# Attention of an encoder layer: probabilities divided by their sum before they are turned, values stationary in two column halves, no turning of the attention output

## What is computed

```python
qb = q.reshape(b, nb, ATTN_BLOCK, g, r, ATTN_HEAD_DIM)
scores = jnp.einsum('bnqgrd,bnkgd->bgrnqk', qb, kb) * (1.0 / math.sqrt(ATTN_HEAD_DIM))
scores = jnp.where(valid, scores - slopes * dist, -jnp.inf)
m = jnp.maximum(jnp.max(scores, axis=-1, keepdims=True), sink_l)
e = jnp.exp(scores - m)
p = e / (jnp.sum(e, axis=-1, keepdims=True) + jnp.exp(sink_l - m))
out = jnp.einsum('bgrnqk,bnkgd->bnqgrd', p, vb)
...
return jnp.concatenate([attn.astype(h.dtype), rec], axis=-1) @ w_out
```

## Time and profile before

| | us |
|---|---|
| median of 3 runs | 1134.76 |
| lowest, highest | 1132.54, 1134.95 |
| the profiled execution | 1135.22 |
| its span in the profile | 1133.4 |
| TensorE busy | 1052.5 (93%) |
| VectorE, ScalarE busy | 306.3 (27%), 174.4 (15%) |
| moved by DMA | 427.89 MB, mean 378 GB/s |

### The profile page before, as it was taken

One profiled execution on the slowest core, in us unless ns is written; L12 is line 12 of the kernel. 1 busy time (PEld: TensorE's weight loads), 2 busy tenths in 40 slices (PEclk: granted clock), 3 DMA queues, 4 the chain that ended last, 5 costly groups with the idle time before them and its releaser, 6 DMA issues.

```text
span 1133.4 us, 14445 instructions
## 1 busy us (share of the span) xinstructions
PE 1052.5 (93%) x5143; PEld 444.2 (39%) x5143; DVE 306.3 (27%) x775; ACT 174.4 (15%) x353; POOL 23.9 (2%) x31
## 2 busy tenths in 40 slices
PE   7999999999999999999999999999999999999996
PEld 6888756333333333333333333333333333332333
DVE  5266344222222222221222222222222222211114
ACT  2263211111111111111111111111111111111101
POOL 2500000000000000000000000000000000000000
PEclk8999999999999999999999999999999999999999
DMA  9722696998999999999999999999999999999992
GB/s 318 207 94 81 270 383 256 389 421 335 422 422 422 422 422 421 421 422 422 422 422 422 422 421 422 422 422 422 422 422 422 422 422 422 421 422 422 422 421 115
DMA packets 73539, 427.89 MB, mean 378 GB/s; under 512 B 8048, under 2 KB 21392, under 8 KB 24272
## 3 DMA queue, kind: packets, MB, share of 16 engines
q1 hardware_dynamic: 71984, 427.19, 92.3%
q10 hardware_dynamic: 1536, 0.43, 0.2%
HBM read 426.02 MB, written 1.05 MB: 377 GB/s over the span
## 4 chain that ended last, share of the span: by engine, by line
PE 56%; DMA 27%; SPq 9%; DVE 6%; issue 2%; ACT 0%; DVEq 0%; ACTq 0%
DMA ring<-in_w_up_dram 26%; PE bank L1308 21%; PE bank L1364 13%; SPq L302 8%; PE bank L1066 8%; PE bank L1273 3%; PE bank L1094 2%; DVE wbuf L991 2%; PE bank L1349 1%; DVE wbuf L986 1%; PE bank L1281 1%; DVE wbuf L995 1%; PE bank L1318 1%; DVE wbuf L985 1%; PE bank L1213 1%
## 5 line engine op out<-in xcount | busy, mean ns | idle before, releaser
L1308 PE MATMUL bank<-ring,wbuf 128*64 128x512 f32 x2032 | 460.6, 595 | 28.8 <-DMA ring<-in_w_up_dram 28.7
L1308 PEld LDWEIGHTS bank<-ring,wbuf 128*64 128x64 f32 x2032 | 140.2, 137 | 324.0 <-issue 224.8
L1364 PE MATMUL bank<-ring,wbuf 128*64 128x512 f32 x960 | 217.5, 595 | 0.0
L985 DVE TENSOR_SCALAR wbuf<-bank 128x256 f32<-128x256 f32 x64 | 26.9, 420 | 361.4 <-PE bank L1308 361.4
L1364 PEld LDWEIGHTS bank<-ring,wbuf 128*64 128x64 f32 x960 | 66.7, 137 | 124.5 <-issue 124.4
L976 DVE TENSOR_SCALAR hT<-iota_s,hT 128x64 f32<-128x64 f32 x62 | 12.9, 251 | 342.1 <-PE bank L1308 342.1
L602 ACT ACTIVATE wbuf<-wbuf 128x256 f32<-128x256 f32 x64 | 26.7, 416 | 506.8 <-DVE wbuf L985 506.8
L963 DVE TENSOR_TENSOR wbuf<-wbuf,bank 128x512 f32<-128x512 f32 x124 | 76.7, 680 | 0.0
L1288 PE MATMUL bank<-wbuf,putT 64*128 64x512 f32 x264 | 65.6, 615 | 0.7 <-ACT wbuf L612 0.7
L1066 PE MATMUL bank<-hT,wbuf 128*128 128x256 f32 x272 | 62.4, 391 | 2.4 <-ACT hT L473 2.4
L1273 PE MATMUL bank<-X,hT 128*64 128x512 f32 x256 | 62.0, 605 | 0.1
(11 more groups left out here) (235 smaller groups left out, 557.2 us busy)
## 6 DMA issues: line engine op xcount, KB each, us to landing
ring<-in_w_up_dram SPq DMA_DIRECT2D x254, 1024.0 KB, 25.2
ring<-in_w_down_dram SPq DMA_DIRECT2D x120, 1024.0 KB, 23.2
wbuf<-in_w_in_dram SPq DMA_DIRECT2D x13, 1024.0 KB, 10.5
wbuf<-in_w_out_dram SPq DMA_DIRECT2D x2, 2048.0 KB, 8.7
wbuf<-in_w_down_dram SPq DMA_DIRECT2D x4, 1024.0 KB, 5.8
mixa<-in_w_up_dram SPq DMA_DIRECT2D x2, 1024.0 KB, 14.5
mixa<-in_w_down_dram SPq DMA_DIRECT2D x2, 1024.0 KB, 9.0
cat<-in_w_down_dram SPq DMA_DIRECT2D x2, 1024.0 KB, 10.5
```

Source lines behind the costliest of these rows:

```text
L985: v.tensor_scalar(glu[:, w], pair[:, :, 0], LIMIT, None, ALU.min).then_inc(s["glu_ready"], 1)
L1308: ins = mm(bank[n][c * SLOTS:(c + 1) * SLOTS, :], xT[:, k, :], wk[:, c * FF + n * 512:c * FF + (n + 1) * 512], start=(k == 0), stop=(k == ...
L1364: ins = mm(bank[2][c * SLOTS:(c + 1) * SLOTS, :], actT[:, at:at + SLOTS], wk[:, a * D + c * 512:a * D + (c + 1) * 512], start=(i == 0 and ...
```

## The change

Each batch's exponentials are multiplied by the reciprocal of their sum on VectorE (`shared`, a 128x1024 product in place in `score`) and only then turned: `pT` waits for the new semaphore `prob_shared` and no longer for `prob_ready`. `shared(b)` stands in VectorE's order where `mixed(b)` stood for b = 0; `shared(1)` comes ahead of `q_in`, `shared(2)` ahead of `scaled(1)`, `shared(3)` ahead of `masked`. `pv` becomes two jobs, one for each token tile: `va` (64 columns of a group) is stationary, `probT` of four heads moves (512 columns), group 0 writes partitions 0 to 63 of the bank, group 1 partitions 64 to 127. The result has the heads' columns on the partitions, so the jobs `catT` 0 and 1 go; ScalarE copies the bank to `attT` (`attended`), and `w_out`'s first half is loaded with its rows in the matching order, in two DMAs of 64 partitions.

```diff
-        STEPS += [("proj", "qh", 0), ("pv", 0, 0), ("proj", "qh", 1)] + two("pT", 1) + two("score", 3)
-        STEPS += [("proj", "ih", 0), ("pv", 1, 0), ("proj", "ih", 1)] + two("pT", 2) + two("kpT", 0)
-        STEPS += [("proj", "zg", 0), ("pv", 2, 0)] + two("kpT", 1) + two("aT", 0) + two("aT", 1) + two("pT", 3)
-        STEPS += [("proj", "zg", 1), ("pv", 3, 0), ("kv", 0, 0), ("kv", 1, 0), ("catT", 0, 0), ("catT", 1, 0)]
+        STEPS += two_of("qh") + two("pT", 1) + two("score", 3)
+        STEPS += [("proj", "ih", 0), ("pv", 0, 0), ("proj", "ih", 1)] + two("pT", 2) + two("kpT", 0)
+        STEPS += [("proj", "zg", 0)] + two("kpT", 1) + two("aT", 0) + two("aT", 1) + two("pT", 3)
+        STEPS += [("proj", "zg", 1), ("pv", 1, 0), ("kv", 0, 0), ("kv", 1, 0)]
...
-            for i in range(2):
-                sp.wait_ge(s["proj_done"], len(UNITS) - 3 + 2 * i)
-                sp.dma_start(wbuf[:, 1 + i, :].rearrange("p (k n) -> p k n", k=4),
-                             w_out_v[:, 4 * i:4 * i + 4, :]).then_inc(s["wout_in"], 16)
-            sp.wait_ge(s["attn_cat"], len(BATCH))
+            sp.wait_ge(s["proj_done"], len(UNITS) - 3)
+            for g in range(NG):
+                sp.dma_start(wbuf[g * DH:(g + 1) * DH, 1, :].rearrange("p (k n) -> p k n", k=QPG),
+                             w_out[0][g * QPG * DH:(g + 1) * QPG * DH, :].rearrange("(k p) n -> p k n", p=DH)).then_inc(s["wout_in"], 16)
+            sp.wait_ge(s["proj_done"], len(UNITS) - 1)
+            sp.dma_start(wbuf[:, 2, :].rearrange("p (k n) -> p k n", k=4), w_out_v[:, 4:8, :]).then_inc(s["wout_in"], 16)
+            for t in range(TT):
+                job_is_read(sp, ("pv", t, 0))
...
+            def attended(t):
+
+                job_is_done(act, ("pv", t, 0))
+                read(a.copy(attT[:, :, t * P:(t + 1) * P],
+                            job_bank(("pv", t, 0))[:, :].rearrange("p (k n) -> p k n", k=QPG)), ("pv", t, 0))
...
             exps(1)
+            attended(0)
             probs(3)
...
             probs_turned(3)
+            attended(1)
             sig_out(0)
             sig_out(1)
...
-            def mixed(b):
-                t, g = BATCH[b]
+            def shared(b):
+
                 dve.wait_ge(s["prob_ready"], b + 1)
                 link(v.tensor_tensor(den[:, b % 2, :], den[:, b % 2, :], es[:, b % 2, :], ALU.add))
                 link(v.reciprocal(rden[:, b % 2, :], den[:, b % 2, :]))
...
+                sc = score[b % 2].rearrange("p (j n) -> p j n", j=QPG)
+                v.tensor_tensor(sc, sc, rden[:, b % 2, :].unsqueeze(2).broadcast_to([P, QPG, TOK]),
+                                ALU.mult).then_inc(s["prob_shared"], 1)
...
             gates(1)
-            mixed(0)
+            shared(0)
             scores(2)
             rescaled(1)
+            shared(1)
             q_in()
             scaled(0)
-            mixed(1)
             scores(3)
+            shared(2)
             scaled(1)
...
-                    pe.wait_ge(s["prob_ready"], d + 1)
+                    pe.wait_ge(s["prob_shared"], d + 1)
...
+                    for g in range(NG):
+                        for hh in range(2):
+                            job_is_read(pe, ("pT", 2 * d + g, hh))
+                    for kt in range(TT):
+                        for g in range(NG):
+                            ins = mm(b[g * DH:(g + 1) * DH, :], va[:, kt, g * DH:(g + 1) * DH],
+                                     probT[g].rearrange("p (j k n) -> p k j n", j=QPG, k=TT)[:, kt, :, :],
+                                     start=(kt == 0), stop=(kt == TT - 1))
```

More of the change, by code:

```diff
@@ L139, in encoder_layer @@
         catm = sb("cat", [P, TT * D])
-        cat = catm[:, :].rearrange("p (t n) -> p t n", t=TT)
+        attT = catm[:, 0:HQ * DH * TT].rearrange("p (k n) -> p k n", n=TOK)
+        rec = catm[:, HQ * DH * TT:].rearrange("p (t n) -> p t n", t=TT)
         mixa = sb("mixa", [P, 4 * NH * TOK])
@@ L202, in encoder_layer @@
                  "wout_in bias_in braw_in bup_split bup_in zeroed consts h_ready lb_ps proj_done job_done logf_ready logf_in exps_in "
-                 "k_ready var_ready std_ready zg_sig mx_ready prob_ready attn_cat rec_cat rms_std mix_half "
+                 "k_ready var_ready std_ready zg_sig mx_ready prob_ready prob_shared rec_cat rms_std mix_half "
                  "mix_done hT_params x1_ready logit_done top_ready g4_ready mask_ready gate_ready "
@@ L516, in probs_turned @@
             def probs_turned(b):
-                if b >= 2:
-                    job_is_done(act, ("pv", b - 2, 0))
+                if b == 2:
+                    job_is_done(act, ("pv", 0, 0))
                 for h in range(2):
@@ L825, in _ @@
             v.tensor_copy(ih[:, 1, :], proj_bank("ih", 1)[:, :]).then_inc(proj_read[GI["ih"]], 1)
-            mixed(2)
+            shared(3)
             masked(0)
             masked(1)
-            mixed(3)
             dve.wait_ge(s["bup_in"], 16)
@@ L847, in _ @@
                     tick(v.scalar_tensor_tensor(
-                        out=cat[:, t, HQ * DH + h * P:HQ * DH + (h + 1) * P],
+                        out=rec[:, t, h * P:(h + 1) * P],
                         in0=job_bank(("o", t, 0))[:, h * P:(h + 1) * P],
@@ L1088, in mix_out @@
                     pe.wait_ge(proj_read[GI["zg" if t == 0 else "ih"]], 1)
-                    pe.wait_ge(s["wout_in"], 32)
+                    pe.wait_ge(s["wout_in"], 48)
                 if n == 0:
-                    for i in ((0, 1), (2 + t,))[part_]:
-                        job_is_read(pe, ("catT", i, 0))
+                    if part_ == 0:
+                        for i in range(TT):
+                            job_is_read(pe, ("pv", i, 0))
+                    else:
+                        job_is_read(pe, ("catT", 2 + t, 0))
                 for k in range(4 * part_, 4 * part_ + 4):
-                    ins = mm(bank[4 + 2 * t + n][:, :], hT[:, k, t * P:(t + 1) * P],
+                    ins = mm(bank[4 + 2 * t + n][:, :], (attT if part_ == 0 else hT)[:, k, t * P:(t + 1) * P],
                              wbuf[:, 1 + k // 4, (k % 4) * D + n * 512:(k % 4) * D + (n + 1) * 512],
@@ L1188, in _ @@
                 elif kind == "catT":
[L1189 to L1194, removed]
+                    pe.wait_ge(s["rec_cat"], d - 1)
+                    ins = turn(b, rec, [(d - 2, k) for k in range(4)])
                 elif kind == "score":
```

## The result

The changed kernel ran in 1136.12 us (median of 18 runs, 1135.18 to 1137.62), the kernel before in 1133.58 (18 runs, 1132.53 to 1135.17). The ratio is 1.0024, with a 95% interval of 1.0016 to 1.0031: slower by 0.24%, with medians 2.5 us apart. The interval holds 0.2%, so the result is clear of zero but not of 0.2%. The forecast was +2.1 us, with a range that holds the result. The profiled execution took 1135.41 us with a span of 1133.7.

What follows compares the result with a forecast made beforehand. The prediction took TensorE's arrival at the experts, which starts the unbroken DMA stream, to set the end. Terms -8.32 + 3.74 + 4.84 = +0.26 us, plus 1.8 for the clock, gave +2.1: median 1136.9 us, range 1133.9 to 1139.0.

Steps and rivals of the forecast that it cites:

- What bounds the kernel: Experts' DMA stream begins when TensorE arrives there; any shift of that arrival shifts the end by as much, either direction.
- What goes: On TensorE's chain: four `pv` jobs, 6.92 us, plus the 1.40 us gap before the second `kv`; 8.32 us saved.
- What comes on TensorE: Two new `pv` jobs at 1.87 us each, taken from the gather's row: 3.74 us, bounds 3.5 and 7.26.
- Rival (c): In the new `pv`, column halves do not run side by side: 7.26 us instead of 3.74, 1140.4 us; chance 0.05.
- The wait ahead of `pT` 0: TensorE waits 4.84 us (bounds 4.3 and 5.9) for batch 0's product, which stands behind `gates(1)` on VectorE.
- rival (d): `pT` 0 does not wait, the product being done before the projection ends: -4.58 us, 1130.2 us; chance 0.05.
- The later batches: Batches 1 to 3 are covered, `pT` 1 with 1.5 us slack; no second wait before `recur` or `mix`.
- The clock: TensorE's clock falls during or just after the `pT` 0 wait: 3.6 us of work at half, 1.8 us lost.
- rival (a): The clock stays at its full level around the `pT` 0 wait: +0.26 us, 1135.0 us; chance 0.28.
- rival (b): Clock falls late in the `pT` 0 wait, staying low under work for 6.9 us: +3.7 us, 1138.4 us; chance 0.07.
- The sum: Whole kernel: work and waits give +0.26 us; with 1.8 us for TensorE's lowered clock, +2.1 us.
- same: Whole kernel's time not told from no change, within about 0.2% or 2.3 us; chance 0.61.

Runs made afterwards that it cites:

- The delay alone: The kernel before with 18 unused identity matmuls ahead of `pT` 0, nothing else changed; ratio 1.0036 to the kernel before.
- The swap: The changed kernel with batch 0's product `shared(0)` ahead of `gates(1)` on VectorE instead of behind it; 1130.74 us, ratio 0.9962 to the kernel before.
- the filled wait: The changed kernel with 18 unused identity matmuls ahead of `pT` 0, filling 4.2 of the 4.9 us wait; ratio 1.0001 to the kernel before.
- the one without the product: The changed kernel with batch 0's product left out, its probabilities going undivided into `pv`; ratio 1.0016 to the kernel before.
- half of the wait filled: The changed kernel with 9 unused identity matmuls ahead of `pT` 0, leaving 2.8 us without work; ratio 1.0011 to the kernel before.

## Why the prediction was right

- **What bounds the kernel.** Right: a shift of TensorE's arrival at the experts is a shift of the end. The delay alone moved the arrival by 4.06 us and the time by 4.1. In the other direction up to 1.8 us more came off the span than off the arrival, which the prediction did not have and no run explains.
- **What goes.** 8.32 us were summed; the chain gives 6.92 + (3.70 - 1.98) = 8.64, as the `kv` jobs without a gap between them also take 0.3 us less.
- **What comes on TensorE.** 3.74 summed, 3.74 measured; the row of the gather carried over exactly. Rival (c) falls. The Trainium skill's advice ("TensorEngine Tiling (Array Packing)", section "When to Use Tiling") to swap the operands and use two column tiles held: 6.92 us became 3.74 for the same products.
- **The wait ahead of `pT` 0.** 4.84 summed, 4.94 measured, and step by step: the product took 1.24 (1.22); the 0.1 more is the step from VectorE to TensorE, 0.14 instead of 0.04. The swap shows the cause, and rival (d), which was the kernel without this wait at -4.58, is about what the swap gave: -4.3 by the ratio, with 0.4 us of wait and slower `pT` 0 left in it, and in its profile a fall of the clock elsewhere.
- **The later batches.** `pT` 1 came at 88.66 with its product done at 85.5, `recur` and `mix` waited for nothing. Right, with more slack than summed, since TensorE lost the clock's time too. `mix` began at 130.01; with the 1.19 us of the quicker start that is 131.2, for the 131.4 expected.
- **The clock.** Right that it falls, and rival (a), a clock that stays up, is the filled wait: +0.1 us measured. The size was right in the profile and the weaker term over the runs. 3.6 us at half were taken and 3.4 measured. `pT` 0 and `score` 2 lost 0.81 + 0.95 = 1.76 us for the 1.8 taken, but 0.2 of that is `pT` 0 after a wait at full clock, which the prediction had not priced; the clock's own part is the 1.56 us against the filled wait. The reason given for 3.6 and not more, that TensorE stood still for a part of the long fall at the start, is not borne out, and that the size agrees is in part luck: ahead of 200 us the ten profiles show falls of about 3.4 us and of about 6.9 us and none between, at the start (six and four of them) as well as at `pT` 0 (three and one), and the long one at `pT` 0 also had 1.3 us without work in it. The runs give 2.6 us for the clock, with an uncertainty of about 1.4. Both profiles of the changed kernel had a short fall, took 1135.41 and 1136.09 us and are among the quicker of their runs, with a mean granted clock of 0.994; all of its runs above 1136.7 us have 0.991. So rival (b), the long fall, probably came true in a part of the executions; it is argued from these means and no trace of such a run shows it.
- **The sum.** In the profile the terms as measured give -8.64 + 3.74 + 4.94 + 1.76 = +1.80, against 1.89 read from zf1 to the experts. +2.1 was forecast, +2.5 measured over the runs (1.8 to 3.5), so the forecast lies inside of the interval. What the runs have more than the profile is probably the clock's term, as said. The measured +2.5 lies on the side of 0.2% to which the prediction gave 0.34, and not on that of "same" with 0.61, but the interval holds the bound between them.

## What to carry to other kernels

Where an engine's order is written by hand, moving an operation ahead of a consumer means to look at its place in the producer's queue: the product cost 1.2 us, the place behind `gates(1)` 3.7. Sum an edit in all the queues, batch by batch, since the first batch, with nothing ahead of it to hide behind, can lose what all of them gain. And price a new wait of TensorE with the clock: here 4.9 us of waiting cost some 7, and when the wait cannot be removed, matmuls without a use in it are worth 1.6 us by the profiles and 2.6 by the runs.

## What was not expected of the hardware

- The clock can fall after a wait has ended: it was at its full level through 4.9 us without work and fell 0.3 us into `pT` 0. The moment is not fixed by the wait: it came 5.2 and 5.4 us after TensorE had stopped in the two profiles of the changed kernel, and 2.4 us after in the one without the product. A look at the clock during the idle time alone would have missed it. The rule of the Trainium skill ("TensorE: Matmul & The Clock Gate", section "HAM oscillation — how this bites in real kernels") that such a wait sends the clock down agrees with the waits of 4.94 and 3.69 us here; the traces add that the fall can come late.
- A fall is not of one length: about 3.4 or about 6.9 us at half of the clock, and no idle time of TensorE seen here tells which. Under work the short one cost 1.56 us.
- Less idle time than was thought was enough in single executions: 2.86 us with half of the wait filled, and in the layer norm a wait of about 1.2 us among transposes and matmuls of 32 columns (one profile of six up to then, 1.6 us lost).
- The clock's return at the start of the kernel, near 16.7 us in one execution and 18.9 in another, moved the end of zf1 by 1.2 us; over the ten profiles that end lies between 66.00 and 67.68. Two profiles of kernels that differ by 0.2% are to be compared from a point behind that: by their spans the change seemed to cost 0.3 us, by the stretch from zf1 to the experts 1.9.
